# First attention: half products ahead of the transposes, reciprocals behind the next maximum, two GpSimd sums by halves

## What is computed

```
s = jnp.einsum('bqkgd,bskd->bkgqs', qi, k) * scale      # qi: one block of 128 queries
p = jax.nn.softmax(s, axis=-1)
return jnp.einsum('bkgqs,bskd->bqkgd', p.astype(v.dtype), v)
```

## Time and profile before

| | |
|---|---|
| median of three runs | 2624.07 us |
| lowest and highest | 2621.78 and 2625.26 us |
| span of the profiled execution | 2619.9 us |
| TensorE matmul | 2539.2 us, 97% of the span, 12946 instructions |
| VectorE | 1587.0 us, 61% |
| ScalarE | 1233.5 us, 47% |
| GpSimd | 1132.0 us, 43% |
| chain that ended last | TensorE 81%, VectorE 10%, ScalarE 5%, issue 2% |

### The profile page before, as it was taken

How to read it: one execution, slowest core, us unless ns; L and a number is a source line. 1 busy time by engine, 2 the same in 40 slices (tenths; PEclk the granted TensorE clock), 3 DMA queues, 4 the chain that set the end, 5 groups by cost and what they waited for, 6 DMA issues and landing times.

```text
span 2619.9 us, 33861 instructions
## 1 busy us (share of the span) xinstructions
PE 2539.2 (97%) x12946; PEld 2112.9 (81%) x12946; DVE 1587.0 (61%) x2413; ACT 1233.5 (47%) x1858; POOL 1132.0 (43%) x754
## 2 busy tenths in 40 slices
PE   5999999999999999999999999999999999999998
PEld 3788788777888888878788888888888888888886
DVE  7654889578555566575833366666666666655333
ACT  4343888445444443333533345543656656652132
POOL 0222434437878774444487334233322222235233
PEclk8999999999999999999999999999999999999999
DMA  6134000432222126553233322222111111157342
GB/s 271 65 121 129 1 1 1 142 101 83 94 77 92 73 100 226 192 177 109 107 113 121 121 73 89 81 69 93 57 53 53 49 49 57 60 206 279 146 185 97
DMA packets 84465, 275.89 MB, mean 105 GB/s; under 512 B 9392, under 2 KB 9520, under 8 KB 84304
## 3 DMA queue, kind: packets, MB, share of 16 engines
q1 hardware_dynamic: 84304, 273.71, 29.8%
HBM read 219.54 MB, written 54.13 MB: 104 GB/s over the span
## 4 chain that ended last, share of the span: by engine, by line
PE 81%; DVE 10%; ACT 5%; issue 2%; POOL 1%; DMA 0%; DVEq 0%; SPq 0%; ACTq 0%; POOLq 0%
PE ps L609 12%; PE ps L611 11%; PE ps L610 11%; PE ps L977 7%; PE ps L978 7%; PE ps L979 7%; PE ps L848 5%; PE ps L829 4%; PE ps L1034 3%; PE ps L1036 3%; PE ps L1035 3%; DVE wf L3047 2%; PE ps L805 2%; PE ps L806 2%; DVE st L2573 1%
## 5 line engine op out<-in xcount | busy, mean ns | idle before, releaser
L3374 POOL TENSOR_TENSOR hl<-raw,hl 128x1024 fp32r<-128x1024 f32 x161 | 403.6, 2509 | 929.9 <-ACT hl L1393 929.9
L609 PE MATMUL ps<-ht,hl 128*128 128x512 f32 x1552 | 633.7, 408 | 10.5 <-DVE ht L2444 5.4
L611 PE MATMUL ps<-ht,hl 128*128 128x512 f32 x1552 | 608.4, 392 | 0.0
L610 PE MATMUL ps<-ht,hl 128*128 128x512 f32 x1552 | 608.2, 392 | 0.0
L609 PEld LDWEIGHTS ps<-ht,hl 128*128 128x128 f32 x1552 | 293.6, 189 | 71.3 <-issue 6.2
L611 PEld LDWEIGHTS ps<-ht,hl 128*128 128x128 f32 x1552 | 293.0, 189 | 63.7
L610 PEld LDWEIGHTS ps<-ht,hl 128*128 128x128 f32 x1552 | 294.0, 189 | 54.2 <-issue 1.7
L3451 POOL TENSOR_SCALAR wf<-wf,st 128x1024 f32<-128x1024 f32 (+2 forms) x192 | 167.9, 874 | 343.1 <-DVE st L2581 287.4
L1393 ACT ACTIVATE hl<-raw 128x1024 fp32r<-128x1024 f32 x163 | 171.4, 1053 | 182.2 <-PE ps L1036 66.5
L2384 DVE TENSOR_TENSOR ps<-ps,wf 128x512 f32<-128x512 f32 x116 | 80.8, 697 | 152.1 <-PE ps L979 151.9
L829 PEld LDWEIGHTS ps<-cst,wf 128*128 128x128 f32 x1088 | 126.6, 141 | 56.2 <-issue 34.4
(11 more groups left out here) (287 smaller groups left out, 5298.5 us busy)
## 6 DMA issues: line engine op xcount, KB each, us to landing
raw<-in_wst SPq DMA_DIRECT2D x243, 512.0 KB, 4.0
wf<-scratch_rows SPq DMA_DIRECT2D x32, 512.0 KB, 5.0
scratch_g<-wf SPq DMA_DIRECT2D x22, 512.0 KB, 2.6
wf<-scratch_g SPq DMA_DIRECT2D x44, 256.0 KB, 4.4
wf<-in_xT SPq DMA_DIRECT2D x16, 512.0 KB, 8.0
htf<-in_wst SPq DMA_DIRECT2D x16, 512.0 KB, 15.4
scratch_ys<-wr SPq DMA_DIRECT2D x16, 512.0 KB, 4.8
ht<-scratch_ys SPq DMA_DIRECT2D x32, 256.0 KB, 6.0
```

The source lines that it names most:

```text
L609: self.op.matmul(out, wh, xh[:, c], start=(j == 0), stop=False)
L610: self.op.matmul(out, wh, xl[:, c], start=False, stop=False)
L611: t = self.op.matmul(out, wl, xh[:, c], start=False, stop=(j == kt - 1))
L3374: self.op.tensor_tensor(K.hl[:, u * 2048 + 1024:u * 2048 + 2048], K.raw[:, i % 3 * 1024:(i % 3 + 1) * 1024], hi.bitcast(F32), ALU.subtract ...
```

## The change

- TensorE: the product of a pair is cut into two halves of eight matmuls. The first half (keys 0 to 3) stands in the odd step two after the pair's last tile, the second (keys 4 to 7) in the even step after it, each between the scores and the transposes of its step. The pairs that end in tiles 61 and 63 are made whole, in steps 63 and 64; the last one goes to bank 7. Ahead of a half's last matmul stands a wait for the low part of the tile before, first half (`ahead`).
- VectorE: the reciprocal of tile s+1 (not s+2 at the step's end) comes behind the maximum of tile s+2, and the addition for the pair of tile s-3 comes behind that, ahead of the subtractions. ScalarE: the copy out for the pair of tile s-3 comes first in its even step.
- GpSimd's sums of squares are made in halves of 512 columns in two steps each.
- Waits that another wait implies are dropped in both attentions (for the maximum where the exponential is waited for, for the high part where the low part is, for the exponential where the reciprocal is, and the like).

```diff
+def product_bank(A, g):
+    return (7, 512) if (A, g) == (1, 63) else (6, 0)
...
# TensorE, scores and turn
-        free = (("top", A, g),) if causal else (("top", A, g), ("exp", A, g))
+        free = (("top", A, g),) if causal else (("exp", A, g),)
...
-            self.emptied[4 + bk] = (("phi", A, g, half), ("plo", A, g, half))
+            self.emptied[4 + bk] = (("plo", A, g, half),)
# TensorE, back
-                self.wait_ge(*K.at("phi", A, gg, half))
                 self.wait_ge(*K.at("plo", A, gg, half))
...
-        self.bank_free(6)
-        for j in range(nk):
+        b, o = product_bank(A, g)
+        js = js or range(nk)
+        if js[0] == 0:
+            self.bank_free(b)
+        for j in js:
             c0 = 128 if causal and j == qt else 0
             for n, m in enumerate((hi, lo)):
-                t = self.op.matmul(K.ps[3][:, c0:256], K.wrr(v)[:, j * 128:(j + 1) * 128],
+                if ahead and (j, n) == (js[-1], 1):
+                    self.wait_ge(*K.at(*ahead))
+                t = self.op.matmul(K.ps[3][:, o + c0:o + 256], K.wrr(v)[:, j * 128:(j + 1) * 128],
...
+        if js[-1] < nk - 1:
+            return
         t.then_inc(*self.done("product", A, g // 2))
# TensorE, attend1
+            if 3 <= s < 65:
+                g, js = s - 2 - (s + 1) % 2, range(4 * ((s + 1) % 2), 4 * ((s + 1) % 2) + 4)
+                if s >= 63:
+                    g, js = 2 * s - 65, range(8)
+                hi, lo, _ = pt1(K, (g // 2) % 2)
+                self.back(1, g, g % 8, hi, lo, 12 + g // 32, False, (("vstack", 1),), js,
+                          ("plo", 1, s - 1, 0))
             if 0 <= s < 64:
                 self.turn(1, s, s % 8, 18 + s % 4, False)
-            if s >= 2 and s % 2 == 0:
-                hi, lo, _ = pt1(K, ((s - 1) // 2) % 2)
-                self.back(1, s - 1, (s - 1) % 8, hi, lo, 12 + (s - 1) // 32, False,
-                          (("vstack", 1),))
# ScalarE, attend1 (its turn and soft follow)
+            if s >= 4 and s % 2 == 0:
+                self.back(1, s - 3, (s - 3) // 8, (s - 3) % 8, K.htlf(4 + (s - 3) // 16))
...
# VectorE, attend1 (top stands ahead, turn behind)
+            if 0 <= s + 1 < 64:
+                self.soft(1, s + 1)
+            if s >= 4 and s % 2 == 0:
+                self.back(1, s - 3, (s - 3) // 8, (s - 3) % 8, K.htlf(4 + (s - 3) // 16))
...
-            if s + 2 < 64:
-                self.soft(1, s + 2)
-            if s >= 2 and s % 2 == 0:
-                h = (s - 1) // 8
-                self.back(1, s - 1, h, (s - 1) % 8, K.htlf(4 + h // 2))
+            if s == 64:
+                self.back(1, 63, 7, 7, K.htlf(7))
# GpSimd, attend1
-            if s in (8, 12, 16):
-                j = s // 4 - 1
+            if s in (8, 9, 12, 13, 16, 17):
+                j, c = s // 4 - 1, HALF[s % 4]
...
-                self.op.tensor_tensor(w(22), w(22), w(23),
+                self.op.tensor_tensor(w(22)[:, c], w(22)[:, c], w(23)[:, c],
```

More of the change, by code:

```diff
@@ L831, in turn, with back @@
             t.then_inc(*self.done("turn", A, g, half))
-            self.emptied[4 + bk] = (("phi", A, g, half), ("plo", A, g, half))
-    def back(self, A, g, qt, hi, lo, v, causal, ready):
+            self.emptied[4 + bk] = (("plo", A, g, half),)
+    def back(self, A, g, qt, hi, lo, v, causal, ready, js=None, ahead=None):
         K = self.K
@@ L843, in back @@
             self.wait_ge(*K.at(*label))
-        self.bank_free(6)
-        for j in range(nk):
+        b, o = product_bank(A, g)
[3 more added lines that the diff above has]
+        for j in js:
             c0 = 128 if causal and j == qt else 0
             for n, m in enumerate((hi, lo)):
-                t = self.op.matmul(K.ps[3][:, c0:256], K.wrr(v)[:, j * 128:(j + 1) * 128],
+                if ahead and (j, n) == (js[-1], 1):
+                    self.wait_ge(*K.at(*ahead))
+                t = self.op.matmul(K.ps[3][:, o + c0:o + 256], K.wrr(v)[:, j * 128:(j + 1) * 128],
                                    m[:, j, c0:256], start=(j == 0 and n == 0),
                                    stop=(j == nk - 1 and n == 1))
+        if js[-1] < nk - 1:
+            return
         t.then_inc(*self.done("product", A, g // 2))
-        self.emptied[6] = (("out", A, g // 2),)
+        self.emptied[b] = (("out", A, g // 2),)
     def attend1(self):
@@ L1632, in soft @@
         pw = K.w(p)[:, 0:nk]
-        self.wait_ge(*K.at("top", A, g))
         if causal:
@@ L1636, in soft @@
         else:
-            self.wait_ge(*K.at("scores", A, g))
+            self.wait_ge(*K.at("top", A, g))
             if g >= 4:
-                for half in (0, 1):
-                    self.wait_ge(*K.at("turn", A, g - 4, half))
+                self.wait_ge(*K.at("turn", A, g - 4, 1))
             else:
                 self.wait_ge(*K.at("tok", 2 if g < 2 else 3))
-        if g >= 16:
-            self.wait_ge(*K.at("weighed", A, g - 16))
         self.op.activation(pw, pw if causal else K.ps[g % 2][:, 0:nk], ACT.Exp, bias=m, scale=1.0,
@@ L1667, in back @@
         self.wait_ge(*K.at("product", A, g // 2))
-        self.op.activation(out[a, c], K.ps[3][0:64, 0:256],
+        o = product_bank(A, g)[1]
+        self.op.activation(out[a, c], K.ps[3][0:64, o:o + 256],
                            ACT.Copy).then_inc(*self.done("outhi", A, g // 2))
@@ L2560, in top @@
         self.wait_ge(*K.at("scores", A, g))
-        if g >= 16:
-            self.wait_ge(*K.at("exp", A, g - 16))
         if causal:
@@ L2593, in turn @@
             r = slice(js[0], js[-1] + 1)
-            self.wait_ge(*K.at("turn", A, g, half))
             self.wait_ge(*K.at("phi", A, g, half))
@@ L2603, in back @@
         self.wait_ge(*K.at("outhi", A, g // 2))
-        self.op.tensor_tensor(out[a, c], K.ps[3][64:128, 0:256], out[a, c],
+        o = product_bank(A, g)[1]
+        self.op.tensor_tensor(out[a, c], K.ps[3][64:128, o:o + 256], out[a, c],
                               ALU.add).then_inc(*self.done("out", A, g // 2))
@@ L3448, in weigh @@
         pw = K.w(p)[:, 0:nk]
-        self.wait_ge(*K.at("exp", A, g))
         self.wait_ge(*K.at("rd", A, g))
@@ L3463, in attend1 @@
                     self.wait_ge(*K.at("toksq", j - 1))
-                self.op.tensor_tensor(w(22), w(22), w(23),
+                self.op.tensor_tensor(w(22)[:, c], w(22)[:, c], w(23)[:, c],
                                       ALU.add).then_inc(*self.done("toksq", j))
-            if s in (43, 50):
-                j = (s - 36) // 7
+            if s in (43, 44, 50, 51):
+                j, c = (s - 36) // 7, HALF[(s - 36) % 7]
                 self.wait_ge(*K.at("attsq1", j))
@@ L3470, in attend1 @@
                     self.wait_ge(*K.at("attsq", j - 1))
-                self.op.tensor_tensor(w(8), w(8), w(9), ALU.add).then_inc(*self.done("attsq", j))
+                self.op.tensor_tensor(w(8)[:, c], w(8)[:, c], w(9)[:, c],
+                                      ALU.add).then_inc(*self.done("attsq", j))
             yield
```

## The result

The changed kernel takes 2604.62 us (median of 4 runs, 2602.37 to 2605.08), the one before 2624.30 (4 runs, 2621.78 to 2625.26): ratio 0.9925, 95% interval 0.9911 to 0.9939, so 19.7 us less. That is inside the forecast range of 2604.5 to 2619, at its very edge (0.1 us above its lower end); the forecast value, 2610, stood for 13.7 us less.

A forecast was written before the change was run, and what follows sets the result against it. TensorE was taken as the bound, stalled once a pair by VectorE's subtraction. 29 pairs of 5.6 (162.4) plus extras made 167.7 against 181.64; with 0.2 back, 13.7 less: 2624.07 to 2610 us, range 2604.5 to 2619.

The forecast's parts named there:

- best case: Whole kernel: 5.55 us a pair, no small waits, dropped waits giving 1 us; 18 us less, 2606.
- The bound and the mechanism: First attention: TensorE's even transposes wait for VectorE's subtraction once a pair; halved products remove this, 6.08 to 5.6 us.
- second rival: First attention: another wait, above all GpSimd's weighing, replaces the removed one; pairs stay at 6.1, 2621 us; chance 0.09.
- third (slower): First attention: loop through reciprocal, weighing, transposes and subtraction exceeds 6.26, about 6.5 us a pair; 2631 us; chance 0.05.
- TensorE's need for a pair: First attention: each step takes scores 1.00, half product 1.00 and transposes 0.79, together 2.79 us; a pair 5.6.
- scores followed by a half have no row: TensorE, first attention: no profile row times a half product behind scores; extra cost taken as 0, bounds -0.05 and 0.1.
- VectorE's list: First attention: VectorE's maxima, reciprocals, subtractions and addition need 5.3 us a pair, fitting 5.6 with 0.3 to spare.
- first rival: First attention: VectorE becomes the bound at 5.9 us a pair, 6.7 us less, 2617; chance 0.24 with part-way cases.
- The weighing: GpSimd, first attention: weighing ends at 5.3, transposes want it at 5.6; ending at least 0.2 before them would show it right.
- Norm work and small waits: First attention: sums 1.9, tables 0.9, squares 0.7, VectorE's copies 0.3, copies and small waits 1.5 us, on top of the pairs.
- Dropped waits: Both attentions: dropping waits that another wait implies gives 0 us, bounds 0 and -2.
- Start and end: First attention: tile 1's transposes 0.7 us later but given back, 0 (bounds -1, +1.5); end +0.2 (bounds 0, 0.6).

The follow-up runs named there:

- halves first and two banks: Against the changed kernel: each half product put ahead of its step's scores, products in banks 6 and 7 by turns; 5.70 us a pair, ratio to the kernel before 0.9954.

## Why the prediction was right, and what was mis-sized

- **The place in the range: partly luck.** The prediction's best case, with nearly all terms good, summed to 18 less (2606); its range went 1.5 us lower for no term that it names, and 2604.62 lies there. The interval of the ratio (0.9911 to 0.9939) is 16 to 23 us less, so another set of runs could have fallen outside.
- **The bound and the mechanism: right.** The transposes' waits for the subtraction are gone from list and chain; whole products bring the stall back at the other tile. The second rival (no change) and the third (slower) did not come about, though a loop near the third's exists: reciprocal, weighing, transposes make 6.7 us a pair when just the reciprocal is moved.
- **TensorE's need for a pair, 5.6: too high by 0.11.** Transposes 0.79 and scores 1.01 are as read. The half product, put at 1.00 by halving the whole one, takes 0.94 behind scores; "scores followed by a half have no row" was bounded at -0.05 and taken as 0. Behind transposes a half takes more: 1.04 in the kernel with the halves first and two banks (352.22 - 351.18). The whole product of the kernel before stood there, and halving it halved that surcharge instead of dropping it. Twice in 29 pairs this is 3.2 us, half of the miss.
- **VectorE's list, 5.3, and its spare: right to 0.1.** It needs 5.36, by rows and by the run with more work on it. The first rival is refuted: operations do start before the last has ended (the reciprocal is 0.15 long, the next operation starts 0.07 behind its start). The Trainium skill, VectorE: DVE Perf Modes, section "The DRAIN you can't avoid", has the next operation wait until the pipe is empty, and adds that one that is not held starts earlier (its next section, "Two Vector instructions with no wait between them"); these rows agree with the addition. But with the pair at 5.49, the spare was 0.13 and not 0.3, so the forecast was nearer to that rival than it knew.
- **The weighing: tighter than reckoned.** It was to end 0.3 ahead of the transposes, with 0.2 as the sign of being right; in the rows above one ends 0.12 ahead and the next 0.46. It held, by less than the forecast thought.
- **Norm work and small waits: nearly right.** 163.31 less 29 x 5.49 leaves 4.1 for sums, tables, squares and copies; forecast 5.3. But the dropped waits are in the 163.31: with them kept, 164.42 leaves 5.2. The sums of 1.84 and the small delays at steps 22 to 26 are there (pairs of 7.28 and 6.27). GpSimd's halves are worth 1.9 us at four places that show it, inside the bounds 0 to 0.7 each.
- **Dropped waits: the step that failed.** "I see no price: 0": the 0.60 between two subtractions with two waits each was a reading of VectorE alone. They cost 1.8 to 2.0 us in the second attention and 1.1 to 1.7 in the first, by the traces of kernels that differ in nothing else: 3 us and more, beyond even the bound of -2. The half products' 3.2, the second attention's 1.9 and the 1.2 of the point above, nearly all of it dropped waits, make 6.3; the measured gain is 6.0 over the forecast 13.7. Why a wait that is met costs time, no run shows.
- **Start and end: as forecast, as far as one trace each shows.** The transposes of tile 1 came 0.6 later (5.78 behind tile 0 instead of 5.18), waiting for GpSimd as reckoned. Tile 0 to tile 4 took 14.78 before and 14.76 after, at a mean granted clock of 0.88 in both: 0, as forecast. The end, tile 62 to the dense layer, took 11.54 before and 11.86 after: +0.3, forecast +0.2.
- **Spans and medians.** The 4.2 us by which the median lay above the span of the kernel before is in all likelihood not what lies around the span, but mostly that execution's place among the runs: for the changed kernel, where the profiled execution's own time is known, 1.8 us lie around it, and 2619.9 + 1.8 is the fastest run of the kernel before.

## What to carry to other kernels

Where two operations of a pipeline take turns unevenly (a large product every second step), look at which steps lack it: the list of waits names the stalled operation, and the same work cut in equal parts can pay for another engine's latency in every step. Reckon each engine's list and each closed loop through several engines for the new order, the emptying of every buffer among them, before moving a step: the reciprocal's move was worth 6 us in one order and cost 14 in the other, and the half products at another place cost 33, of which 27 for want of a second bank. Waits that another wait implies have a price here, 3 us in all, even where the profile shows no idle time for them; drop them.

## What the runs showed of the hardware

- Implied waits: 1.8 to 2.0 us over 128 tiles of the second attention, with TensorE busy in 298.37 of 300 us there before and 299.17 of 300 after. Which engine's waits cost it was not tried apart.
- Eight matmuls of 128x256 take 0.94 us behind scores of 128x512 and 1.04 behind transposes; sixteen behind transposes take 1.99.
- Operations of VectorE overlap: the next one starts 0.07 us after the start of a reciprocal of 0.15 us, and 1.13 us after that of a maximum of 1.22 us.
- After 3.2 to 3.8 us without work TensorE may run at 1.2 GHz for a while (matmuls of 128x512 start 0.43 apart instead of 0.23) or not, with the same code up to there: mean granted clock 0.77 and 15.37 us, or 1.00 and 13.67 us, over tile 0 to tile 4. The one trace that kept its full clock there lost 1.6 us to the lower level at step 22.
